# Layer 1 of a two-layer mixer block: the two products of a w_hi tile joined into one of 512 columns

## The reference

```python
hx = modulate(rms_norm(x, g_mix[l]), sh1, sc1)            # (256, 1024)
px = split_cols(hx @ w_in[l], IN_SIZES)                   # q, k, v, conv, gated conv, fourier, 4 gates
...                                                       # attention, two conv branches, a 2-D DFT
m = sum(sigmoid(gate_i) * (y_i @ w_br_i) for i in range(4))
x = x + gt1 * (m @ w_out[l])
h = modulate(rms_norm(x, g_ffn[l]), sh2, sc2)
a, b = jnp.split(h @ w_up[l], 2, axis=-1)                 # 2 x 2816 columns
x = x + gt2 * ((silu(dwconv3(a)) * b) @ w_down[l])
```

## Time and profile before

| | |
|---|---|
| median of 3 runs | 1321.76 us |
| profiled execution, own time | 1320.71 us |
| its span (first to last instruction) | 1318.9 us |
| TensorE matmul busy | 1266.8 us (96%), 7661 matmuls |
| weight load busy | 1096.6 us (83%) |
| VectorE busy | 883.2 us (67%) |
| ScalarE busy | 550.7 us (42%) |
| GpSimd busy | 286.8 us (22%) |
| mean granted TensorE clock | 0.984 of full speed |
| chain that ended last | PE 77%, DVE 14%, issue 4%, ACT 4% |

### The profile page before, as it was taken

The page is one execution under the profiler, slowest core; times in us unless marked ns, Lnnn a source line. Parts: engine busy times, 40 slices in busy tenths (PEclk is TensorE's granted clock), DMA queues, the critical chain, the costliest instruction groups (busy, mean ns, idle before and its releaser), DMA issues.

```text
span 1318.9 us, 19887 instructions
## 1 busy us (share of the span) xinstructions
PE 1266.8 (96%) x7661; PEld 1096.6 (83%) x7661; DVE 883.2 (67%) x1203; ACT 550.7 (42%) x870; POOL 286.8 (22%) x247
## 2 busy tenths in 40 slices
PE   5999999999999999998999999999989998999997
PEld 3788777778788788887888888889878998999997
DVE  5694488652898669994766664576586667665654
ACT  4322345653423334331233332344556645653543
POOL 0003499110242001111001120003771130210210
PEclk8999999999999989998999999999999998999999
DMA  9463221212466415664655664335333553564561
GB/s 378 168 202 118 74 73 68 68 54 91 137 196 227 128 47 186 197 202 154 201 162 190 191 213 141 97 102 175 119 105 108 176 176 128 191 217 138 188 208 33
DMA packets 50339, 198.76 MB, mean 151 GB/s; under 512 B 5584, under 2 KB 6992, under 8 KB 49104
## 3 DMA queue, kind: packets, MB, share of 16 engines
q1 hardware_dynamic: 50256, 197.62, 45.4%
HBM read 196.55 MB, written 1.05 MB: 150 GB/s over the span
## 4 chain that ended last, share of the span: by engine, by line
PE 77%; DVE 14%; issue 4%; ACT 4%; DMA 0%; DVEq 0%; ACTq 0%; SPq 0%
PE psA L511 22%; PE psA L512 21%; PE psA L513 21%; DVE w_lo L1220 3%; DVE ada_sum L1241 3%; ACT w_hi L935 2%; PE psB L513 2%; PE psB L511 2%; PE psB L512 2%; DVE acc L1462 2%; DVE small L1475 1%; PE psA L753 1%; PE psB L781 1%; PE psB L769 1%; PE psB L684 1%
## 5 line engine op out<-in xcount | busy, mean ns | idle before, releaser
L511 PE MATMUL psA<-h_hi,w_hi 128*128 128x256 f32 (+1 forms) x1544 | 525.5, 340 | 11.4 <-DVE h_lo L1340 4.9
L512 PE MATMUL psA<-h_lo,w_hi 128*128 128x256 f32 (+1 forms) x1544 | 518.4, 336 | 0.0
L513 PE MATMUL psA<-h_hi,w_lo 128*128 128x256 f32 (+1 forms) x1544 | 518.2, 336 | 0.0
L1220 DVE TENSOR_TENSOR w_lo<-raw,w_hi 128x1024 fp32r<-128x1024 f32 (+2 forms) x244 | 335.4, 1375 | 135.1 <-ACT w_hi L935 135.0
L935 ACT ACTIVATE w_hi<-raw 128x1024 fp32r<-128x1024 f32 (+2 forms) x244 | 277.2, 1138 | 335.6 <-PE psA L513 230.2
L511 PEld LDWEIGHTS psA<-h_hi,w_hi 128*128 128x128 f32 x1544 | 297.3, 193 | 44.7 <-issue 9.5
L513 PEld LDWEIGHTS psA<-h_hi,w_lo 128*128 128x128 f32 x1544 | 297.2, 193 | 29.0
L512 PEld LDWEIGHTS psA<-h_lo,w_hi 128*128 128x128 f32 x1544 | 297.3, 193 | 28.1 <-issue 0.2
L500 POOL TENSOR_TENSOR hid_lo<-sig,hid_hi 128x512 f32 (+3 forms) x44 | 68.0, 1545 | 485.8 <-ACT hid_hi L1184 485.8
L1241 DVE SCALAR_TENSOR_TENSOR ada_sum<-raw,csil,ada_sum 128x1024 f32<-128x1024 f32 x112 | 159.2, 1452 | 0.0
L511 PE MATMUL psA<-hid_hi,w_hi 128*128 128x256 f32 (+1 forms) x352 | 118.9, 338 | 6.3 <-DVE w_lo L1220 4.0
(11 more groups left out here) (190 smaller groups left out, 1421.5 us busy)
## 6 DMA issues: line engine op xcount, KB each, us to landing
raw<-w_up SPq DMA_DIRECT2D x88, 512.0 KB, 4.2
raw<-w_ada SPq DMA_DIRECT2D x80, 512.0 KB, 3.6
raw<-w_dn SPq DMA_DIRECT2D x32, 704.0 KB, 4.9
raw<-w_in SPq DMA_DIRECT2D x36, 512.0 KB, 4.1
raw<-w_at SPq DMA_DIRECT2D x24, 512.0 KB, 3.6
raw<-w_fn SPq DMA_DIRECT2D x16, 640.0 KB, 3.9
raw<-w_sc SPq DMA_DIRECT2D x16, 640.0 KB, 3.9
raw<-w_cf SPq DMA_DIRECT2D x16, 640.0 KB, 4.0
```

The source lines that it names most:

```text
L511: pe.matmul(out, w0, hi, start=first, stop=False)
L512: pe.matmul(out, w0, lo, start=False, stop=False)
L513: return pe.matmul(out, w1, hi, start=False, stop=last)
L1220: dve.tensor_tensor(w_lo[:, s, 0:tiles * P], raw[:, r, 0:tiles * P], w_hi[:, s, 0:tiles * P].bitcast(F32), ALU.subtract).then_inc(rest_don ...
```

## The change

In layer 1, h_hi and h_lo (and mg, hid) become two halves of one tensor, and the w_hi tile is multiplied by both at once, 512 columns, the first half of the bank getting w_hi h_hi and the second w_hi h_lo. The w_lo product of 256 columns goes to the first half. Whoever reads the bank must add the halves. Joined are ten of the 18 chunks of `in` (0 to 3, 6, 7, 8, 10, 12, 13), and all of `out`, `up0`, `dn0`, `up1`, `dn1`. Layer 0 and the branch stages stay. The core of the diff:

```diff
-        h_hi = place("h_hi", [KD, NT], F32R)
-        h_lo = place("h_lo", [KD, NT], F32R)
+        h_two = place("h_two", [2, KD, NT], F32R)
+        h_hi, h_lo = h_two[:, 0, :, :], h_two[:, 1, :, :]
...
+            def pair_product(bank, st, tile, two, first, last):
+                w0 = w_hi[:, st.slot, tile * P:(tile + 1) * P]
+                w1 = w_lo[:, st.slot, tile * P:(tile + 1) * P]
+                wide_out = bank[:, :].rearrange("p (a t) -> p a t", a=2)
+                if not last:
+                    pe.matmul(wide_out, w0, two, start=first, stop=False)
+                mm = pe.matmul(bank[:, 0:SEQ], w1, two[:, 0, :], start=False, stop=False)
+                if last:
+                    mm = pe.matmul(wide_out, w0, two, start=first, stop=True)
+                return mm
+
+            def chunk_product(layer, st, kk, two, cols, first, last):
+                if layer:
+                    return pair_product(psA[st.slot], st, kk, two[:, :, kk, cols], first, last)
+                return product(psA[st.slot][:, cols], st, kk, two[:, 0, kk, cols], two[:, 1, kk, cols], first, last)
...
@@ ScalarE, up stages, even chunk: middle tap
-                            act.wait_ge(chunk_done, st.up(st.n + 1))
+                            if layer:
+                                act.wait_ge(joined, st.up(JOINED[f"up{f}"] + st.idx + 1))
+                            else:
+                                act.wait_ge(chunk_done, st.up(st.n + 1))
                             act.wait_ge(evac, st.up(st.n - 2))
-                            act.activation(tmp[b][:, 0:T], psA[st.slot][:, 0:T], ACT.Identity,
+                            act.activation(tmp[b][:, 0:T], tmp[b][:, T:2 * T] if layer else psA[st.slot][:, 0:T],
+                                           ACT.Identity,
...
+            def gather(st, dst):
+                bank = psA[st.slot]
+                if st.n < PER_LAYER:
+                    return dve.tensor_copy(dst, bank[:, 0:NT])
+                return dve.tensor_reduce(dst, bank[:, :].rearrange("p (a t) -> p t a", a=2), AX.X, ALU.add)
...
@@ VectorE, in stage, one of the chunks (tensor_copy of 256 columns becomes gather)
-                        dve.tensor_copy(f_in(layer, idx - 6), ps[:, 0:T]).then_inc(evac, 1)
+                        gather(st, f_in(layer, idx - 6)).then_inc(evac, 1)
...
@@ VectorE, residual (out, dn0, dn1), ahead of line 1623
+                            if layer:
+                                src = X[:, bass.ds(o, 1), cols].rearrange("p a t -> p (a t)")
+                                g = mod[:, layer, bass.ds(o + ada_col, 1), s:s + 1].rearrange("p a b -> p (a b)")
+                                dve.scalar_tensor_tensor(src, bank[:, SEQ:NT], g, src, ALU.mult, ALU.add)\
+                                    .then_inc(joined, 1)
+                                dve.wait_ge(joined, st.up(JOINED[name] + st.idx + 1))
...
@@ VectorE, up stages
                         dve.wait_ge(chunk_done, st.up(st.n + 1))
+                        if layer:
+                            gather(st, tmp[b][:, T:2 * T] if st.idx % 2 == 0 else sig[b][:, T:2 * T])\
+                                .then_inc(joined, 1)
+                            ps = (tmp if st.idx % 2 == 0 else sig)[b][:, T:2 * T]
...
@@ VectorE, odd chunk, after the waits for silu and hid_rest
+                            if layer:
+                                dve.wait_ge(joined, st.up(JOINED[f"up{f}"] + st.idx + 1))
                             dve.tensor_tensor(sig[b][:, 0:T], ps, tmp[b][:, 0:T], ALU.mult).then_inc(evac, 1)
```

More of the change, by code:

```diff
@@ L100 @@
 AT_ORDER = [(0, 0), (0, 1), (1, 0), (1, 1), (0, 2), (2, 0), (2, 1), (1, 2), (3, 0), (3, 1), (2, 2), (3, 2)]
+JOINED_IN = (0, 1, 2, 3, 6, 7, 8, 10, 12, 13)
+JOINED, _j = {}, 0
+for _name in ("out", "up0", "dn0", "up1", "dn1"):
+    JOINED[_name] = _j
+    _j += LEN[_name]
 VEC, _at = {}, 0
@@ L219, in program @@
         assert top[0] <= nc.sbuf_usable_end, (top[0], nc.sbuf_usable_end)
-        mg_hi = at("mg_hi", [KD, NT], F32R, y_off)
-        mg_lo = at("mg_lo", [KD, NT], F32R, y_off + 4 * KD * NT)
+        mg_two = at("mg_two", [2, KD, NT], F32R, y_off)
+        mg_hi, mg_lo = mg_two[:, 0, :, :], mg_two[:, 1, :, :]
         assert y_off + 4 * NT * 2 * HALF_FF <= t_off
-        hid_hi = at("hid_hi", [HALF_FF, NT], F32R, y_off)
-        hid_lo = at("hid_lo", [HALF_FF, NT], F32R, y_off + 4 * HALF_FF * NT)
+        hid_two = at("hid_two", [2, HALF_FF, NT], F32R, y_off)
+        hid_hi, hid_lo = hid_two[:, 0, :, :], hid_two[:, 1, :, :]
         x_in = at("x_in", [KD, NT], F32, q_off)
@@ L290, in program @@
         m_sum, m_head, m_rest = map(sem, ("m_sum", "m_head", "m_rest"))
+        joined = sem("joined")
         cv, silu, hid_head, hid_rest, fin = map(sem, ("cv", "silu", "hid_head", "hid_rest", "fin"))
@@ L567, in reduction_read, with lead @@
                     pe.wait_ge(mod_done, POS[REDUCE[st.n - late]] + 1)
-            def lead(layer, name, T, count, hi, lo, ready, r=None):
+            def lead(layer, name, T, count, two, ready, r=None):
                 first = layer * PER_LAYER + START[name]
@@ L582, in lead @@
                         for st in sts:
-                            mm = product(psA[st.slot][:, cols], st, kk, hi[:, kk, cols], lo[:, kk, cols],
-                                         kk == 0, kk == count - 1)
+                            mm = chunk_product(layer, st, kk, two, cols, kk == 0, kk == count - 1)
                             if kk == count - 1 and s == len(splits) - 1:
@@ L690, in _ @@
                 if layer:
-                    lead(layer, "in", T, KD, h_hi, h_lo, (h_rest, 32 * layer), 2 * layer)
+                    lead(layer, "in", T, KD, h_two, (h_rest, 32 * layer), 2 * layer)
                 for idx in range(AHEAD if layer else FIRST_LEAD, LEN["in"]):
@@ L713, in _ @@
                     cols = NT if idx in (4, 5) else T
-                    from_h(st, cols, psA[st.slot][:, 0:cols]).then_inc(chunk_done, 1)
+                    if layer and idx in JOINED_IN:
+                        for kk in range(KD):
+                            mm = chunk_product(layer, st, kk, h_two, slice(0, T), kk == 0, kk == KD - 1)
+                        mm.then_inc(chunk_done, 1)
+                    else:
+                        from_h(st, cols, psA[st.slot][:, 0:cols]).then_inc(chunk_done, 1)
                     reduction_read(st, 1)
@@ L883, in project @@
                     for kk in range(KD):
-                        mm = product(psA[st.slot][:, 0:T], st, kk, mg_hi[:, kk, 0:T], mg_lo[:, kk, 0:T],
-                                     kk == 0, kk == KD - 1)
+                        mm = chunk_product(layer, st, kk, mg_two, slice(0, T), kk == 0, kk == KD - 1)
                     mm.then_inc(chunk_done, 1)
                     reduction_read(st, 1)
-                lead(layer, "out", T, KD, mg_hi, mg_lo, (m_rest, 8 * layer))
+                lead(layer, "out", T, KD, mg_two, (m_rest, 8 * layer))
                 walk(pe, layer, "out", project, lead=AHEAD)
@@ L896, in lift @@
                         begin(st)
-                        from_h(st, T, psA[st.slot][:, 0:T]).then_inc(chunk_done, 1)
+                        for kk in range(KD):
+                            mm = chunk_product(layer, st, kk, h_two, slice(0, T), kk == 0, kk == KD - 1)
+                        mm.then_inc(chunk_done, 1)
                         reduction_read(st, 1)
@@ L900, in _ @@
                     if f == 0:
-                        lead(layer, "up0", T, KD, h_hi, h_lo, (h_rest, 16 * (2 * layer + 1)),
+                        lead(layer, "up0", T, KD, h_two, (h_rest, 16 * (2 * layer + 1)),
                              2 * layer + 1)
@@ L913, in lower @@
                         for c in range(HALF_FF):
-                            mm = product(psA[st.slot][:, 0:T], st, c, hid_hi[:, c, 0:T], hid_lo[:, c, 0:T],
-                                         c == 0, c == HALF_FF - 1)
+                            mm = chunk_product(layer, st, c, hid_two, slice(0, T), c == 0, c == HALF_FF - 1)
                         mm.then_inc(chunk_done, 1)
@@ L918, in _ @@
                     name = f"dn{f}"
-                    lead(layer, name, T, HALF_FF, hid_hi, hid_lo, (hid_rest, HALF_FF * (2 * layer + f)))
+                    lead(layer, name, T, HALF_FF, hid_two, (hid_rest, HALF_FF * (2 * layer + f)))
                     walk(pe, layer, name, lower, lead=AHEAD, skip=LEN[name] if layer == 0 else 0)
@@ L1311, in query @@
                 dve.wait_ge(chunk_done, st.n + 1)
-                dve.tensor_copy(q[:, st.idx, 0:T], psA[st.slot][:, 0:T]).then_inc(evac, 1)
+                gather(st, q[:, st.idx, 0:T]).then_inc(evac, 1)
             def norm(layer, which):
@@ L1419, in _ @@
                     elif idx < 8:
-                        dve.tensor_copy(f_in(layer, idx - 6), ps[:, 0:T]).then_inc(evac, 1)
+                        gather(st, f_in(layer, idx - 6)).then_inc(evac, 1)
```

(4 more changed lines are left out.)

1 line of the change is left out of this document (added).

## The result

The changed kernel takes 1340.2 us (median of 4 runs, 1338.94 to 1342.32) against 1322.18 us of before in the same runs: ratio 1.014, 95% interval 1.0126 to 1.0153. It is slower, by 18 us; 10.9 us were forecast (1332.6 us, in a range of 1321 to 1342 us).

What follows compares the result with a forecast made beforehand. TensorE bounds the kernel now; after the change VectorE would bind in `up`. Terms -0.95 + 1.7 + 6.7 - 1.2 + 2.0 + 1.3 - 1.2 + 2.0 + 0.5 = +10.9 us: 1332.6 us, range 1321 to 1342 us.

Steps and rivals of the forecast that it cites:

- the clock falls behind each stall: Start of `dn0` and `dn1`: lower granted clock after TensorE's stall costs 2.0 us each, with ends 0 and 2.4 us.
- Rival A: In `up`, TensorE stays the bound and gets faster: -6.0 us, 1315.8 us; chance 0.08.
- C: Rival: VectorE's gather in `up` takes 1.36 us, adding 27 us, 1360 us; chance 0.04.
- D: Rival: VectorE binds as forecast, but the clock holds at the `dn` starts: 1328.6 us; chance 0.16.
- B: Rival: the gather goes by its outputs, 0.42 us, pair 5.30 us: +0.3 us, 1322.0 us; chance 0.07.
- the pair of the loop on VectorE: In `up`, two chunks take VectorE 5.82 us, against TensorE's 5.55 us; `dn0` starts 6.7 us later, `up1` adds 1.3 us.
- the 90% that I named as a sign: Sign of the forecast: VectorE is busy for about 90% of `up`.
- TensorE's gain: Joined tiles in layer 1: 0.0133 us less each, 672 tiles, 8.9 us if TensorE remained the bound throughout.
- rival E: The wide matmul gains nothing; `in` and `dn` give back 3.3 us, the rest follows VectorE: 1336 us; chance 0.05.
- `out`: In `out`, VectorE's step goes from 1.86 to 2.38 us with a second residual; the norm comes 1.7 us later.
- `in`: In `in`, joined tiles make the stage 0.95 us shorter; VectorE has about 0.5 us to spare at each chunk.
- The tail: At the end of `dn1` the last residual is double: 0.5 us more.

Runs made afterwards that it cites:

- e5: Changed kernel, with TensorE running 8 and 6 float32 matmuls of constants in the layer 1 stalls ahead of `dn0` and `dn1`: 1336.12 us, ratio 1.0099 to before.
- e2: Changed kernel, but ScalarE's middle tap in `up` reads a ready piece of h and does not wait for the gather: 1325.45 us, ratio 1.003 to before.
- e1: Changed kernel's joined matmuls, but readers as before, first half of the bank only, no gather or second residual: 1317.94 us against 1322.11 us before, ratio 0.9963.
- e11: As e1, but outside `lead` a chunk's wide and narrow matmuls are grouped, the last wide one at the end: 1314.72 us (one run).
- e9: Joined only ten chunks of `in`, first 5 of `out`, `dn0`, first 7 of `dn1`, odd chunks of `up`: 1318.87 us against 1322.96 us before, ratio 0.9961.
- e12: As e9, with wide and narrow matmuls grouped: 1318.91 us against 1321.77 us of the kernel before, ratio 0.9977.
- e3: Changed kernel, but in even chunks of `up`, except first and last, VectorE gathers before making w_lo: 1332.36 us, ratio 1.008 to before.

## Why the prediction held, point by point

- **Direction and mechanism.** Right. VectorE binds in `up`, TensorE stalls ahead of `dn` (forecast 7.4 and 4.7 us, measured 7.70 and 5.90 us) and the clock falls behind each stall (forecast 2.0 us each; e5: 1.26 and 2.23 us). e2 shows that the order gather, then tap is what binds. Rival A (TensorE stays the bound), C (a gather of 1.36 us) and D (the clock holds) are out by the rows. B is out by the gather's own 0.685 us (line 1346, mean of 22).
- **The size.** +10.9 us forecast; layer 1 and the tail measured +16.0 us in the profile (the table without layer 0), +18 us in the timed runs. The step that was mis-sized is the pair of the loop on VectorE: 5.82 us forecast, 6.14 us measured. Its terms: middle tap from SBUF 0.60 us, not the 0.51 us of line 981 (line 1227 reads a scale per channel besides the bias; 22 of them with a median of 0.602 us against 40 of line 981 with 0.508 us); handoff gather to tap 0.17 and 0.31 us, not 0.12 us; product to w_lo 0.52 us in one pair of two (1162.50 to 1163.02), not 0.34 us. The six pairs in each loop make 1.6 and 1.2 us, the pair ahead of the loop 0.4 us (6.00 us, not 5.57 us), the others together 0.4 and 0.5 us: 2.4 us in `up0` (61.2 us from the first tap to that of chunk 20, not 58.8 us) and 2.2 us in `up1` (60.5 us, not 58.3 us). In `up0` the first tap ends 10.7 us behind the first matmul, not 11.5 us, in a profile where 3.0 us of the stage's start were at the lower clock and not 5.3 us as before; without that bit of luck its miss of 1.6 us would have been 2.4 us. VectorE's busy share in `up0` is 78%, not the 90% that I named as a sign: of the 6.32 us of the pair shown 1.08 us are the wait for the tap alone. These two pairs were off by 0.32 us; the six of the loop were off by 0.26 us in the mean in `up0` and by 0.21 us in `up1`, about the 0.25 us to which I trusted the pair. The Trainium skill, "ScalarE: Activation LUTs", section on what ACT_TABLE_LOAD costs, puts each operand read from a [128,1] pointer at about 93 ns; the two medians are 94 ns apart, so the trace agrees, and I should have looked at the operands and not at the tile alone.
- **TensorE's gain.** 13.3 ns a tile forecast from the earlier trace rows, 7 to 8 ns measured in e1. I took spacings from streams of one width; wide and narrow in turn run slower (e11). In `up` this cost nothing here, since VectorE bound; `dn` lost some 0.5 us each. So rival E, that the wide matmul gains nothing, was true in part.
- **`out`.** Right: VectorE's step is 2.38 us as forecast (1100.98 to 1103.36 in its timeline), the norm 1.83 us later. Not seen: the low clock now comes before the norm's spread, and its four small matmuls take 1.22 us at a granted clock of 0.50 (1115.21) and not 0.71 us (1111.26 before), +0.5 us between spread and `up0`.
- **`in`.** -0.90 us against -0.95, but the second profile of before has 76.87 us, which makes it -0.3 us. At equal clock (7.5 us of `in` at the lower one before, 6.2 us before again, 6.6 us after) both come to about -0.5 us, an estimate at 0.5 us for each us; 80 tiles at 7 to 8 ns are 0.6 us. That the figure of the table meets the forecast is luck.
- **The tail.** +1.0 us against +0.5: 0.6 us up to the norm's spread, which is the double residual (e9 and e12, without it, have a tail of 10.1 us), and 0.4 us behind it, where the spread's matmuls again take 1.22 us and not 0.71 us.
- **Left open.** The timed runs show 2 us more than layer 1's stretches. With layer 0 varying by 2 us a profile can't place it.

## What to carry to other kernels

Work that moves from the engine that binds to one with spare time is free only where its result is read late: the spare time of VectorE in `up` was a wait in a chain, and the new instruction went into that chain. Ask of each reader whether it lies in a chain between two engines; here joining the odd chunks of `up` alone was a gain, and joining the even ones as well, whose gather has the tap behind it, a loss. A stage that hands over with a group of chunks shows every lag of the slower engine at once, and a long stall of TensorE costs the low clock on top: ahead of `dn`, idle times of 3.5 to 7.7 us were all followed by it (e2, e3 and the changed kernel), those of 1.0 to 1.4 us never.

## What the runs showed of the hardware

- Matmuls of 512 and 256 columns in turn take 0.351 us a pair in `up1` (61.81 us over 176 tiles, with the boundaries), where the sum of the spacings in streams of one width is 0.347 us; grouped by width 0.348 us (61.22 us).
- A moving operand of two runs of 256 columns costs the same as one of 512 (61.81 and 61.78 us for the stage, one profile each).
- Float32 matmuls of constants in a stall of 7.70 us hold the granted clock at 1.00 behind it; without them it is 0.60 over 3.53 us, and 0.50 over 3.25 us behind the stall of 5.90 us. It is worth 1.26 and 2.23 us.
- A reduction of 512 PSUM elements over pairs 256 apart to 256 outputs takes 0.685 us, as much as a copy of 512 (0.691 us in the earlier trace rows).
- VectorE's left tap of 255 elements takes 0.92 to 0.97 us where it overlaps GpSimd's subtraction of 256 elements (14 times in e3) and 0.48 us where it doesn't (8 times).
